# Sixty-four gathered row operations spread over a matmul pass, the final add and scale cut into halves, and four slots for rounded blocks

## The chip, the cores and the metric

The kernel runs on one core of a Trainium2 chip. The metric is the device time of one execution in microseconds (us); lower is better. The names of the engines are those of the profile: PE is TensorE (PEld its weight loads), DVE is VectorE, ACT is ScalarE, POOL is GpSimd, SP is SyncE.

## The reference, cut to what matters

The whole is one decoder layer over 256 tokens of width 2048: three attention branches, an output projection, and then a channel mixer with a table of 16384 experts, and a last RMSNorm. Only the mixer's value side and the norm are touched:

```python
def peer_ffn(h, w_q, sub_keys, u_tab, v_tab):
    ...                      # 8 heads x 16 chosen experts for each token: experts, g
    def chunk(args):
        xc, ec, gc = args
        a = jax.nn.gelu(jnp.einsum("td,thkd->thk", xc, u_tab[ec]))
        return jnp.einsum("thk,thkd->td", gc * a, v_tab[ec])
...
x = x + peer_ffn(rmsnorm(x, g_ffn[l]), ...)
return rmsnorm(x, g_final)   # y = x * rsqrt(mean(x*x) + EPS) * g
```

## The kernel before

The tokens are two tiles of 128 (t = 0 and 1), and a tile's (head, 16 experts) pairs are units, 16 in all. For 12 units the coefficient of each chosen expert is put into a dense matrix `ct` of 128 x 128 coefficients per token, and their value side is a dense product, the value pass: all 16384 rows of the table `peer_v` are read in 128 blocks of 128 rows. For the 4 last units, all of tile 1, the rows are gathered instead, 16 of `peer_u` and 16 of `peer_v` for each token and unit: 128 late operations, numbered n = 0 to 127. The first 64 are dot products (L1413), the last 64 add a gathered row times its coefficient to the residual `x1f[1]` (L1419). Here they are called dots and row operations. They stand inside the value pass.

In the value pass, for a block b:

- SP issues the load of block b into `v_raw[b % 4]` (L560) once block b-4 is used up (`acc_ok`).
- ACT rounds it to `v_hi` (L1064) and the coefficients to `c_hi` (L1087). `v_hi` and `c_hi` have two slots (`NHL`), so ACT waits until block b-2 is used up: `wait(act, acc_ok, b - 1)`.
- DVE subtracts: `v_lo` (in the place of `v_raw`, L1424), `c_lo` (L1426), and then does the late operations that the table `OPS_AT` gives to block b.
- PE does 24 matmuls of 128x512 (L1761): for each token tile t, for each of four column groups c, the three products hi*hi, hi*lo, lo*hi. All eight PSUM banks accumulate over the 128 blocks. Blocks 4 to 123 are a loop of four blocks a turn.
- POOL issues the gather of late operation n into one of four row slots (L641) when operation n-4 is done.

The table gives operation n >= 12 to block n + 4, and what would lie beyond block 127 to a last entry, which DVE works off behind its loop:

```python
for n in range(2 * LATE_OPS):
    b = n + n // 3 if n < 12 else min(n + 4, PKEYS)
    OPS_AT[b].append(n)
```

So operation 123 is in block 127, and 124 to 127 stand behind the loop. Then comes the end: for each tile DVE adds PSUM to `x1f[t]` (L1443, 2048 columns, on `fin_pe`), ACT squares and sums it (L1096), DVE and ACT work out 1/sqrt(mean + EPS) from it in small operations (L1107 to L1117 on DVE, L702 on ACT), and DVE multiplies into `outst[t]` in two halves (L1448), which SP stores (L582). At block 35 SP also loads the residuals of both tiles into `x1f` (L575).

Of the kernel before, what the change touches and what calls it, by code (L numbers as in the profile page):

```python
# [44 lines left out]
PH, PKEYS, PTOP = 8, 128, 16  # L45
EPS = 1e-6
# [20 lines left out]
NRAW, NHL = 4, 2  # L67
# [26 lines left out]
RING = 4  # L94
# [4 lines left out]
LATE_GROUPS = PTOP * (N_EARLY - PH) // GTOK  # L99
LATE_OPS = N_LATE * PTOP  # L100
V_FEW = 16
OPS_AT = {b: [] for b in range(PKEYS + 1)}
for n in range(2 * LATE_OPS):
    b = n + n // 3 if n < 12 else min(n + 4, PKEYS)
    OPS_AT[b].append(n)


# [80 lines left out]
def build(nc, x, rel_bias, g_mix, w_in, a_sinks, c_lat_gain, c_w_uk, c_w_uv, w_br_a, w_br_b, w_br_c,  # L188
# [5 lines left out]
    def at(name, kib, shape, dt=F32):  # L194
        return nc.alloc_sbuf_tensor_at(name, shape, dt, offset=base + int(kib * K))
# [24 lines left out]
    stat = at("stat", 205.0625, [P, 7, 8])  # L220
# [34 lines left out]
    ct = at("ct", 0, [P, NT, PKEYS, P])  # L255
# [35 lines left out]
    pickT = at("pickT", 205.46875, [P, 3, P])  # L291
    iota_f = at("iota_f", 206.96875, [P, P])

    ROW_AT, V_AT, VH_AT = (128, 168, 0, 64), (176, 192, 184, 160), (144, 152)
    row_ring = [at(f"row_ring{i}", kib, [P, D]) for i, kib in enumerate(ROW_AT)]
    v_raw = [at(f"v_raw{i}", kib, [P, D]) for i, kib in enumerate(V_AT)]
    v_lo = [at(f"v_lo{i}", kib, [P, D], FR) for i, kib in enumerate(V_AT)]
    v_hi = [at(f"v_hi{i}", kib, [P, D], FR) for i, kib in enumerate(VH_AT)]
    c_hi = [at(f"c_hi{i}", kib, [P, NT, P], FR) for i, kib in enumerate((205.46875, 202.0625))]
    c_lo = [at(f"c_lo{i}", kib, [P, NT, P], FR) for i, kib in enumerate((206.46875, 204))]  # L300
    x1f = [at(f"x1f{t}", kib, [P, D]) for t, kib in enumerate((72, 8))]
    gfin = at("gfin", 16, [P, D])
    outst = [at(f"outst{t}", kib, [P, D]) for t, kib in enumerate((80, 24))]

    ps = ctx.enter_context(nc.psum_tensor("ps", [P, 8, 512], F32))
    J, S_BANK, O_BANK, T_BANK, PT_BANK = 0, 2, 4, 5, 6
# [20 lines left out]
    lo_done = sem("lo_done")  # L327
    blk_done = sem("blk_done")
    evac_done = sem("evac_done")
    SSQ = {0: 1, 1: 2, 2: 3, 5: 4, 6: 5}  # L330
    sq_ok = sem("sq_ok")
    ssq_ok = sem("ssq_ok")
    ve_ok = sem("ve_ok")
    rt_ok = sem("rt_ok")
# [63 lines left out]
    ch_ok = sem("ch_ok")  # L398
# [26 lines left out]
    vh_ok = sem("vh_ok")  # L425
# [6 lines left out]
    o_ok = sem("o_ok")  # L432
# [255 lines left out]
    def _(act):  # L688
# [371 lines left out]

        def high_v(b):
            act.wait_ge(v_in[b % RING], 16 * (b // RING + 1))
            wait(act, acc_ok, b - 1)
            nc.scalar.activation(v_hi[b % NHL][:, :], v_raw[b % RING][:, :], ACT.Copy).then_inc(vh_ok, 1)  # L1064

        for b in range(NHL):
            high_v(b)
# [16 lines left out]
        for b in range(PKEYS):  # L1084
            if b >= NHL:
                high_v(b)
            nc.scalar.activation(c_hi[b % NHL][:, :, :], ct[:, :, b], ACT.Copy).then_inc(ch_ok, 1)  # L1087
            for n in OPS_AT[b - 1] if b else ():
                if n < LATE_OPS and n % PTOP == PTOP - 1:
                    squared(N_EARLY + n // PTOP)  # L1090
                    tanh_of(N_EARLY + n // PTOP)

        nc.scalar.activation(one_root[:, :], one_col[:, :], ACT.Sqrt)
        for t in range(NT):
            act.wait_ge(sum_ok, t + 1)
            nc.scalar.activation(outst[t][:, :], x1f[t][:, :], ACT.Square, accum_out=stat[:, 5 + t, 0:1]).then_inc(ssq_ok, 1)  # L1096
            root(5 + t, 1)


# [1 line left out]
    def _(dve):  # L1101
        def mean_root(q, cols, count, summed=False):

            s = stat[:, q]
            if not summed:
                dve.wait_ge(ssq_ok, SSQ[q])
            nc.vector.tensor_scalar(s[:, 2:2 + cols], s[:, 0:cols], 1.0 / count, EPS, ALU.mult, ALU.add).then_inc(ve_ok, 1)  # L1107
            dve.wait_ge(rt_ok, q + 1)
            nc.vector.reciprocal(s[:, 6:6 + cols], s[:, 4:4 + cols])
            dve.drain()  # L1110
            nc.vector.tensor_tensor(s[:, 4:4 + cols], s[:, 6:6 + cols], s[:, 6:6 + cols], ALU.mult)
            dve.drain()
# [328 lines left out]
        for t in range(NT):
            dve.wait_ge(fin_pe, t + 1)
            nc.vector.tensor_tensor(x1f[t][:, :], x1f[t][:, :], ps[:, 4 * t:4 * t + 4, :].rearrange("p a b -> p (a b)"), ALU.add).then_inc(sum_ok, 1)  # L1443
        for t in range(NT):
            mean_root(5 + t, 1, D)
            for h in range(2):
                cols = slice(D // 2 * h, D // 2 * (h + 1))
                nc.vector.scalar_tensor_tensor(out=outst[t][:, cols], in0=x1f[t][:, cols], scalar=stat[:, 5 + t, 6:7], in1=gfin[:, cols],  # L1448
                                               op0=ALU.mult, op1=ALU.mult).then_inc(o_ok, 1)


    @block.tensor
    def _(pe):
# [319 lines left out]


# [21 lines left out]
```

## Time and profile before

| what | us |
|---|---|
| median of 3 runs | 2097.63 |
| lowest and highest run | 2091.3, 2100.59 |
| the profiled execution | 2097.23 |
| its span | 2095.9 |

The span is the part of the profiled execution between its first and last recorded instruction. Times in the profile count from the span's start. The value pass begins at 1351.7 us and its last matmul at 2073.89 us. Clocks of PE are given as a share of full speed. An idle time in square brackets stands before an instruction, with what ended it.

### The profile page before, as it was taken

How to read it: one execution, taken by the hardware profiler on the slowest of the kernel's cores; microseconds unless marked ns; L12 is line 12 of the kernel's file. 1: busy time of each engine (PE TensorE's matmuls, PEld its weight loads, DVE VectorE, ACT ScalarE, POOL GpSimd, SP SyncE). 2: the span in 40 equal slices, each digit the busy share in tenths (PEclk: the TensorE clock that was granted, in tenths of full speed). 3: DMA queues.
4: the chain of work that ended last, by engine and by line, in shares of the span. 5: the costliest groups of instructions: out<-in, count | busy, mean ns of one | idle time of the engine just before them, and what ended most of it. 6: DMA issues, size and time to landing. Idle time of an engine off the chain costs nothing.

```text
span 2095.9 us, 27844 instructions
## 1 busy us (share of the span) xinstructions
PE 1790.6 (85%) x10780; PEld 1590.0 (76%) x10780; DVE 1551.0 (74%) x2043; ACT 856.1 (41%) x1312; POOL 477.7 (23%) x438
## 2 busy tenths in 40 slices
PE   7999999999999989656655235699999999999995
PEld 6999999999998877555644234588878888888884
DVE  5464444444565449999999999877878888888988
ACT  5444444444443421022222877534334334343342
POOL 0000000010053013453333767012211222212211
PEclk9999999999999999877877555799999999999998
DMA  9555555555467569989999899289999999999995
GB/s 312 158 168 168 168 170 171 171 171 166 143 189 281 191 232 418 422 363 426 392 382 395 336 397 426 96 333 351 393 378 367 392 375 381 381 380 372 369 387 212
DMA packets 293540, 627.82 MB, mean 300 GB/s; under 512 B 10365, under 2 KB 223406, under 8 KB 234959
## 3 DMA queue, kind: packets, MB, share of 16 engines
q0 software_dynamic: 48400, 343.95, 40.9%
q1 hardware_dynamic: 244558, 282.20, 39.5%
q8 instruction: 47, 0.77, 0.1%
q10 hardware_dynamic: 496, 0.58, 0.1%
q14 instruction: 39, 0.31, 0.0%
HBM read 622.45 MB, written 8.44 MB: 301 GB/s over the span
## 4 chain that ended last, share of the span: by engine, by line
PE 66%; DVE 19%; DVEq 5%; issue 4%; DMA 3%; ACT 1%; POOL 1%; another core or an unknown queue 1%; SPq 0%; POOLq 0%; ACTq 0%
PE ps L1761 33%; PE ps L1464 23%; DVE u_ring L1346 10%; DVEq L1301 4%; PE ps L1624 4%; PE ps L1646 2%; DMA u_ring<-in_peer_u,idx_all 2%; DMA v_raw<-in_peer_v 1%; DVE ones_d L1378 1%; DVE ones L1378 1%; PE ps L1569 1%; PE ps L1550 1%; PE ps L1559 0%; DVE pick L1334 0%
## 5 line engine op out<-in xcount | busy, mean ns | idle before, releaser
L1123 DVE TENSOR_TENSOR w_lo<-raw,w_hi 128x2048 fp32r<-128x2048 f32 x112 | 259.1, 2313 | 331.2 <-ACT w_hi L697 331.1
L1464 PE MATMUL ps<-act_hi,w_hi 128*128 128x256 f32 x1536 | 440.3, 287 | 4.9 <-DVE act_lo L1248 2.9
L1464 PE MATMUL ps<-act_hi,w_lo 128*128 128x256 f32 x1536 | 434.6, 283 | 0.0
L1464 PE MATMUL ps<-act_lo,w_hi 128*128 128x256 f32 x1536 | 434.5, 283 | 0.0
L1064 ACT ACTIVATE v_hi<-v_raw 128x2048 fp32r<-128x2048 f32 x128 | 245.3, 1917 | 423.6 <-PE ps L1761 414.9
L1761 PE MATMUL ps<-v_hi,c_hi 128*128 128x512 f32 x1024 | 406.6, 397 | 6.7 <-DVE c_lo L1426 6.7
L1761 PE MATMUL ps<-v_hi,c_lo 128*128 128x512 f32 x1024 | 405.5, 396 | 0.0
L1761 PE MATMUL ps<-v_lo,c_hi 128*128 128x512 f32 x1024 | 403.3, 394 | 0.0
L1346 DVE CUSTOM_DVE_ANT_0 u_ring<-u_ring,ps 128x2048 f32<-128x2048 f32 x159 | 359.8, 2277 | 14.6 <-DMA u_ring<-in_peer_u,idx_all 14.3
L1424 DVE TENSOR_TENSOR v_lo<-v_raw,v_hi 128x2048 fp32r<-128x2048 f32 x128 | 293.7, 2294 | 94.1 <-ACT v_hi L1064 94.0
L697 ACT ACTIVATE w_hi<-raw 128x2048 fp32r<-128x2048 f32 x112 | 214.1, 1911 | 262.5 <-PE ps L1464 217.8
L1464 PEld LDWEIGHTS ps<-act_hi,w_hi 128*128 128x128 f32 x1536 | 294.5, 192 | 6.1 <-issue 4.0
L1464 PEld LDWEIGHTS ps<-act_lo,w_hi 128*128 128x128 f32 x1536 | 294.6, 192 | 0.3 <-issue 0.2
L1464 PEld LDWEIGHTS ps<-act_hi,w_lo 128*128 128x128 f32 x1536 | 294.4, 192 | 0.0
L641 POOL DMA_INDIRECT u_ring<-in_peer_u,idx_all x192 | 187.8, 978 | 285.8 <-DVE early_dots L1346 198.8
L1761 PEld LDWEIGHTS ps<-v_hi,c_hi 128*128 128x128 f32 x1024 | 192.8, 188 | 54.2 <-DVE c_lo L1426 4.9
L1761 PEld LDWEIGHTS ps<-v_lo,c_hi 128*128 128x128 f32 x1024 | 192.8, 188 | 47.7
L1761 PEld LDWEIGHTS ps<-v_hi,c_lo 128*128 128x128 f32 x1024 | 192.9, 188 | 44.3
L1419 DVE SCALAR_TENSOR_TENSOR x1f<-row_ring,cw_all,x1f 128x2048 f32<-128x2048 f32 x64 | 150.5, 2351 | 6.9 <-issue 0.9
L641 POOL DMA_INDIRECT row_ring<-in_peer_u,idx_all x64 | 73.6, 1150 | 338.1 <-DVE late_dots L1413 321.8
L1413 DVE CUSTOM_DVE_ANT_0 row_ring<-row_ring,h 128x2048 f32<-128x2048 f32 x64 | 146.2, 2284 | 0.0
L641 POOL DMA_INDIRECT row_ring<-in_peer_v,idx_all x64 | 81.3, 1270 | 277.9 <-DVE x1f L1419 257.7
(225 smaller groups left out, 2095.5 us busy)
## 6 DMA issues: line engine op xcount, KB each, us to landing
v_raw<-in_peer_v SPq DMA_DIRECT2D x128, 1024.0 KB, 7.0
raw<-in_w_in SPq DMA_DIRECT2D x80, 1024.0 KB
raw<-in_w_out SPq DMA_DIRECT2D x16, 1024.0 KB
wq_raw<-in_peer_w_q SPq DMA_DIRECT2D x8, 2048.0 KB, 19.0
raw<-in_w_br_a SPq DMA_DIRECT2D x16, 512.0 KB
bias_by_query<-bias_by_distance POOLq DMA_DIRECT2D x1, 4096.0 KB, 21.1
bias_st<-bias_by_query POOLq DMA_DIRECT2D x16, 256.0 KB, 4.7
raw<-in_w_br_b SPq DMA_DIRECT2D x16, 256.0 KB
```

What stands on the lines that cost most here:

```text
L641: return pool.indirect_dma_start(dst, None, table, bass.IndirectOffsetOnAxis(ap=idx_all[:, PTOP * unit + k:PTOP * unit + k + 1], axis=0))
L697: nc.scalar.activation(w_hi[:, j % NHL], raw[:, j % NRAW], ACT.Copy).then_inc(hi_done, 1)
L1064: nc.scalar.activation(v_hi[b % NHL][:, :], v_raw[b % RING][:, :], ACT.Copy).then_inc(vh_ok, 1)
L1123: nc.vector.tensor_tensor(w_lo[:, j % NHL], raw[:, j % NRAW], w_hi[:, j % NHL].bitcast(F32), ALU.subtract).then_inc(lo_done, 1)
L1301: dve.drain()
L1346: nc.vector.tensor_tensor_reduce(out=u_ring[:, slot], in0=u_ring[:, slot], in1=h2p[u // PH], scale=0.5, scalar=0.0, op0=ALU.mult, op1=ALU. ...
L1413: nc.vector.tensor_tensor_reduce(out=row_ring[slot][:, :], in0=row_ring[slot][:, :], in1=h2[:, 1], scale=0.5, scalar=0.0, op0=ALU.mult, op ...
L1419: nc.vector.scalar_tensor_tensor(out=x1f[1][:, :], in0=row_ring[slot][:, :], scalar=cw_all[:, PTOP * unit + k:PTOP * unit + k + 1], in1=x1 ...
L1424: nc.vector.tensor_tensor(v_lo[b % RING][:, :], v_raw[b % RING][:, :], v_hi[b % NHL][:, :].bitcast(F32), ALU.subtract)
L1464: last = nc.tensor.matmul(out_ap, w_parts[wp][:, slot, k], act_parts[ap][:, k], start=(k == k0 and m == 0), stop=(k == k1 - 1 and m == 2))
L1624: last = nc.tensor.matmul(ps[:, 2 * (c % 2) + t, :], mg_parts[ap][:, T * k + P * t:T * k + P * t + P], w_wide[wp][:, j % NHL, kk], start=( ...
L1761: last = nc.tensor.matmul(ps[:, 4 * t + c, :], c_parts[cp][j % NHL][:, t], v_parts[vp][j % v_slots[vp]][:, WIDE * c:WIDE * c + WIDE], star ...
```

## The change

The table gives operations 64 to 127 places that come 0 to 6 blocks earlier, `n + 4 - (n - 64) // 10`: every ninth block from 77 on (77, 86, 95, 104, 113, 122) takes two row operations instead of one, the last operation is in block 125, and none stands behind the loop. From block 64 on `v_hi`, `c_hi` and `c_lo` have four slots instead of two; the new ones lie where coefficients of used-up blocks were. PE's loop over the blocks becomes two loops, one for each count of slots. The output tiles move to places of row slots 0 and 1. At the end `fin_pe` counts half tiles, DVE adds half tiles, ACT squares half tiles into two sums, and DVE's small operations are put in between; one of them fewer stands in the root, and one more in the mean.

```diff
-OPS_AT = {b: [] for b in range(PKEYS + 1)}
+OPS_AT = {b: [] for b in range(PKEYS)}
 for n in range(2 * LATE_OPS):
-    b = n + n // 3 if n < 12 else min(n + 4, PKEYS)
+    b = n + n // 3 if n < 12 else n + 4 - max(n - LATE_OPS, 0) // 10
     OPS_AT[b].append(n)
...
-    ROW_AT, V_AT, VH_AT = (128, 168, 0, 64), (176, 192, 184, 160), (144, 152)
+    ROW_AT, V_AT, VH_AT = (128, 168, 0, 64), (176, 192, 184, 160), (144, 152, 80, 24)
...
-    c_hi = [at(f"c_hi{i}", kib, [P, NT, P], FR) for i, kib in enumerate((205.46875, 202.0625))]
-    c_lo = [at(f"c_lo{i}", kib, [P, NT, P], FR) for i, kib in enumerate((206.46875, 204))]
+    c_hi = [at(f"c_hi{i}", kib, [P, NT, P], FR) for i, kib in enumerate((205.46875, 202.0625, 88, 89))]
+    c_lo = [at(f"c_lo{i}", kib, [P, NT, P], FR) for i, kib in enumerate((206.46875, 204, 90, 91))]
...
-    outst = [at(f"outst{t}", kib, [P, D]) for t, kib in enumerate((80, 24))]
+    outst = [at(f"outst{t}", kib, [P, D]) for t, kib in enumerate((128, 168))]
...
+    def hi_slot(b):
+
+        return b % NHL if b < PKEYS // 2 else b % RING
+
...
-            wait(act, acc_ok, b - 1)
-            nc.scalar.activation(v_hi[b % NHL][:, :], v_raw[b % RING][:, :], ACT.Copy).then_inc(vh_ok, 1)
+            wait(act, acc_ok, b - 1 if b < PKEYS // 2 + NHL else max(b - RING + 1, PKEYS // 2))
+            nc.scalar.activation(v_hi[hi_slot(b)][:, :], v_raw[b % RING][:, :], ACT.Copy).then_inc(vh_ok, 1)
...
-            act.wait_ge(sum_ok, t + 1)
-            nc.scalar.activation(outst[t][:, :], x1f[t][:, :], ACT.Square, accum_out=stat[:, 5 + t, 0:1]).then_inc(ssq_ok, 1)
+            for h in range(2):
+                cols = slice(D // 2 * h, D // 2 * (h + 1))
+                act.wait_ge(sum_ok, 2 * t + h + 1)
+                nc.scalar.activation(outst[t][:, cols], x1f[t][:, cols], ACT.Square, accum_out=stat[:, 5 + t, h:h + 1]).then_inc(ssq_ok, 1)
             root(5 + t, 1)
...
-        for n in OPS_AT[PKEYS]:
-            late_op(n)
...
+        def add_half(t, h):
+
+            cols = slice(D // 2 * h, D // 2 * (h + 1))
+            dve.wait_ge(fin_pe, 2 * t + h + 1)
...
+        add_half(0, 0)
+        add_half(0, 1)
+        add_half(1, 0)
+        mean_square(0)
+        add_half(1, 1)
+        inverse_root(0)
+        out_half(0, 0)
+        mean_square(1)
+        out_half(0, 1)
+        inverse_root(1)
+        out_half(1, 0)
+        out_half(1, 1)
...
-        add_block(0, first=True)
-        with pe.Fori(1, PKEYS // RING - 1) as i:
-            add_block(i)
-        add_block(PKEYS // RING - 1, final=True)
+        add_block(0, (NHL, RING), first=True)
+        with pe.Fori(1, PKEYS // RING // 2) as i:
+            add_block(i, (NHL, RING))
+        with pe.Fori(PKEYS // RING // 2, PKEYS // RING - 1) as i:
+            add_block(i, (RING, RING))
+        add_block(PKEYS // RING - 1, (RING, RING), final=True)
```

The first place is DVE around block 77, operations 72 to 75. The digit in a name is its slot: `x1f1` is the residual of tile 1, `row_ring0` to `row_ring3` are the row slots. Before:

```order
L1419 SCALAR_TENSOR_TENSOR x1f1_155<-row_ring0_136,cw_all_118,x1f1_155 128x2048 [waits row_in0]
L1424 TENSOR_TENSOR v_lo1_145<-v_raw1_141,v_hi1_149 128x2048 [waits vh_ok]
L1426 TENSOR_TENSOR c_lo1_153<-ct_99,c_hi1_151 128x256 [waits ch_ok]
L1419 SCALAR_TENSOR_TENSOR x1f1_155<-row_ring1_137,cw_all_118,x1f1_155 128x2048 [waits row_in1]
L1424 TENSOR_TENSOR v_lo2_146<-v_raw2_142,v_hi0_148 128x2048 [waits vh_ok]
L1426 TENSOR_TENSOR c_lo0_152<-ct_99,c_hi0_150 128x256 [waits ch_ok]
L1419 SCALAR_TENSOR_TENSOR x1f1_155<-row_ring2_138,cw_all_118,x1f1_155 128x2048 [waits row_in2]
```

After:

```order
L1425 SCALAR_TENSOR_TENSOR x1f1_161<-row_ring0_136,cw_all_118,x1f1_161 128x2048 [waits row_in0]
L1430 TENSOR_TENSOR v_lo1_145<-v_raw1_141,v_hi1_149 128x2048 [waits vh_ok]
L1432 TENSOR_TENSOR c_lo1_157<-ct_99,c_hi1_153 128x256 [waits ch_ok]
L1425 SCALAR_TENSOR_TENSOR x1f1_161<-row_ring1_137,cw_all_118,x1f1_161 128x2048 [waits row_in1]
L1425 SCALAR_TENSOR_TENSOR x1f1_161<-row_ring2_138,cw_all_118,x1f1_161 128x2048 [waits row_in2]
L1430 TENSOR_TENSOR v_lo2_146<-v_raw2_142,v_hi2_150 128x2048 [waits vh_ok]
L1432 TENSOR_TENSOR c_lo2_158<-ct_99,c_hi2_154 128x256 [waits ch_ok]
```

Two row operations stand between the `c_lo` of block 77 and the `v_lo` of block 78, and block 78 has slot 2 of `v_hi` instead of slot 0.

The second place is DVE at the end of its program, from the `v_lo` of block 127 to the last output. Before:

```order
L1424 TENSOR_TENSOR v_lo3_147<-v_raw3_143,v_hi1_149 128x2048 [waits vh_ok]
L1426 TENSOR_TENSOR c_lo1_153<-ct_99,c_hi1_151 128x256 [waits ch_ok]
L1419 SCALAR_TENSOR_TENSOR x1f1_155<-row_ring3_139,cw_all_118,x1f1_155 128x2048 [waits row_in3]
L1419 SCALAR_TENSOR_TENSOR x1f1_155<-row_ring0_136,cw_all_118,x1f1_155 128x2048 [waits row_in0]
L1419 SCALAR_TENSOR_TENSOR x1f1_155<-row_ring1_137,cw_all_118,x1f1_155 128x2048 [waits row_in1]
```

After (the row operation at the top is 127, in block 125):

```order
L1425 SCALAR_TENSOR_TENSOR x1f1_161<-row_ring3_139,cw_all_118,x1f1_161 128x2048 [waits row_in3]
L1430 TENSOR_TENSOR v_lo2_146<-v_raw2_142,v_hi2_150 128x2048 [waits vh_ok]
L1432 TENSOR_TENSOR c_lo2_158<-ct_99,c_hi2_154 128x256 [waits ch_ok]
L1430 TENSOR_TENSOR v_lo3_147<-v_raw3_143,v_hi3_151 128x2048 [waits vh_ok]
L1432 TENSOR_TENSOR c_lo3_159<-ct_99,c_hi3_155 128x256 [waits ch_ok]
```

Five row operations, 123 to 127, stood between the last `c_lo` and the first add (the last two of them are left out above), and now none does. The operations in the adds' and outputs' part stand in the order that the diff's last twelve calls on DVE show.

## Rows read from the trace of the kernel before

**Rows 1.** The page: span, and its chain that ended last, by line.

```profile
span 2095.9 us, 27844 instructions
...
PE ps L1761 33%; PE ps L1464 23%; DVE u_ring L1346 10%; DVEq L1301 4%; PE ps L1624 4%; PE ps L1646 2%; DMA u_ring<-in_peer_u,idx_all 2%; DMA v_raw<-in_peer_v 1%; DVE ones_d L1378 1%; DVE ones L1378 1%; PE ps L1569 1%; PE ps L1550 1%; PE ps L1559 0%; DVE pick L1334 0%
```

**Rows 2.** The chain in order of time, from 1380 us: start, length, what.

```profile
1379.80 158.35 PE ps L1761 x679
...
1538.17 16.61 DMA v_raw<-in_peer_v
...
1559.42 503.72 PE ps L1761 x2160
```

**Rows 3.** Timeline of DVE, end of the value pass and after it.

```profile
2065.18 2.29 DVE L1424 TENSOR_TENSOR v_lo<-v_raw,v_hi 128x2048 fp32r<-128x2048 f32 x1 [0.49 <-ACT v_hi L1064]
2067.39 0.42 DVE L1426 TENSOR_TENSOR c_lo<-ct,c_hi 128x256 fp32r<-128x256 f32 x1
2067.90 9.68 DVE L1419 SCALAR_TENSOR_TENSOR x1f<-row_ring,cw_all,x1f 128x2048 f32<-128x2048 f32 x4
2078.00 2.35 DVE L1419 SCALAR_TENSOR_TENSOR x1f<-row_ring,cw_all,x1f 128x2048 f32<-128x2048 f32 x1 [0.42 <-DMA row_ring<-in_peer_v,idx_all]
2080.44 4.48 DVE L1443 TENSOR_TENSOR x1f<-x1f,ps 128x2048 f32<-128x2048 f32 x2
...
2089.59 0.16 DVE L1109 RECIPROCAL stat<-stat 128x1 f32<-128x1 f32 x1 [0.27 <-ACT stat L702]
2089.83 0.16 DVE L1111 TENSOR_TENSOR stat<-stat 128x1 f32<-128x1 f32 x1
...
2090.76 2.48 DVE L1448 SCALAR_TENSOR_TENSOR outst<-x1f,stat,gfin 128x1024 f32<-128x1024 f32 x2
```

**Rows 4.** Timeline of PE at three matmuls of the last two blocks.

```profile
2062.74 0.40 PE L1761 MATMUL ps<-v_lo,c_hi 128*128 128x512 f32 x1
...
2068.57 0.40 PE L1761 MATMUL ps<-v_hi,c_hi 128*128 128x512 f32 x1
...
2073.89 0.39 PE L1761 MATMUL ps<-v_lo,c_hi 128*128 128x512 f32 x1
```

**Rows 5.** Timeline of ACT: the last rounding, a square, its sum, a root.

```profile
2063.23 1.92 ACT L1064 ACTIVATE v_hi<-v_raw 128x2048 fp32r<-128x2048 f32 x1 [3.33 <-PE ps L1761]
...
2082.76 1.91 ACT L1096 ACTIVATE outst<-x1f 128x2048 f32<-128x2048 f32 x1 [15.79 <-DVE x1f L1443]
2084.58 0.19 ACT L1096 ACTIVATION_READ_ACCUMULATOR outst<-x1f 128x1 f32 x1
...
2089.36 0.20 ACT L702 ACTIVATE stat<-stat 128x1 f32<-128x1 f32 x1 [2.24 <-DVE stat L1107]
```

**Rows 6.** Groups of DVE by line, 1740 to 2096 us.

```profile
L1419 DVE SCALAR_TENSOR_TENSOR x1f<-row_ring,cw_all,x1f 128x2048 f32<-128x2048 f32 x64 | 150.5, 2351 | 6.9 <-issue 0.9 <-DMA row_ring<-in_peer_v,idx_all 0.4
L1424 DVE TENSOR_TENSOR v_lo<-v_raw,v_hi 128x2048 fp32r<-128x2048 f32 x59 | 135.5, 2296 | 28.4 <-ACT v_hi L1064 28.3
```

**Rows 7.** Loads of `v_raw` issued from 1700 us on: issue to landing.

```profile
DMA to landing us min/median/max: 4.7/6.9/9.8
```

**Rows 8.** Gathers into `row_ring`, 1740 to 2060 us: issue to landing.

```profile
DMA to landing us min/median/max: 5.4/7.4/12.1
```

**Rows 9.** Stretches: length, busy times, PE clock, DMA share, GB/s.

```profile
1745.00:2067.00 322.00, 322.00 (x1388) 259.98 (x1387) 288.09 (x173) 130.28 (x118) 69.52 (x58) 1.00 0.95 372
...
1534.00:1556.00 22.00, 20.93 (x90) 16.50 (x88) 14.55 (x12) 6.50 (x7) 3.79 (x4) 1.00 1.00 417
```

**Rows 10.** Timeline of PE around its one wait in the pass.

```profile
1554.53 0.40 PE L1761 MATMUL ps<-v_lo,c_hi 128*128 128x512 f32 x1
1559.42 0.50 PE L1761 MATMUL ps<-v_hi,c_hi 128*128 128x512 f32 x1 [4.49 <-DVE c_lo L1426]
...
1560.08 0.63 PE L1761 MATMUL ps<-v_lo,c_hi 128*128 128x512 f32 x1
1560.51 0.63 PE L1761 MATMUL ps<-v_hi,c_hi 128*128 128x512 f32 x1
```

More of the change, by code:

```diff
@@ L329, in build @@
     evac_done = sem("evac_done")
-    SSQ = {0: 1, 1: 2, 2: 3, 5: 4, 6: 5}
+    SSQ = {0: 1, 1: 2, 2: 3, 5: 5, 6: 7}
     sq_ok = sem("sq_ok")
@@ L1086, in _ @@
                 high_v(b)
-            nc.scalar.activation(c_hi[b % NHL][:, :, :], ct[:, :, b], ACT.Copy).then_inc(ch_ok, 1)
+            nc.scalar.activation(c_hi[hi_slot(b)][:, :, :], ct[:, :, b], ACT.Copy).then_inc(ch_ok, 1)
             for n in OPS_AT[b - 1] if b else ():
@@ L1423, in _ @@
             dve.wait_ge(vh_ok, b + 1)
-            nc.vector.tensor_tensor(v_lo[b % RING][:, :], v_raw[b % RING][:, :], v_hi[b % NHL][:, :].bitcast(F32), ALU.subtract)
+            nc.vector.tensor_tensor(v_lo[b % RING][:, :], v_raw[b % RING][:, :], v_hi[hi_slot(b)][:, :].bitcast(F32), ALU.subtract)
             dve.wait_ge(ch_ok, b + 1)
-            nc.vector.tensor_tensor(c_lo[b % NHL][:, :, :], ct[:, :, b], c_hi[b % NHL][:, :, :].bitcast(F32), ALU.subtract).then_inc(vl_ok, 1)
+            nc.vector.tensor_tensor(c_lo[hi_slot(b)][:, :, :], ct[:, :, b], c_hi[hi_slot(b)][:, :, :].bitcast(F32), ALU.subtract).then_inc(vl_ok, 1)
             for n in OPS_AT[b - 2] if b > 1 else ():
@@ L1440, in _ @@
         dve.drain()
[L1441 to L1449, printed above, removed]
+        def add_half(t, h):
+            cols = slice(D // 2 * h, D // 2 * (h + 1))
+            dve.wait_ge(fin_pe, 2 * t + h + 1)
+            nc.vector.tensor_tensor(x1f[t][:, cols], x1f[t][:, cols], ps[:, 4 * t + 2 * h:4 * t + 2 * h + 2, :].rearrange("p a b -> p (a b)"),
+                                    ALU.add).then_inc(sum_ok, 1)
@@ new lines, in mean_square, with inverse_root @@
+        def mean_square(t):
+            s = stat[:, 5 + t]
+            dve.wait_ge(ssq_ok, SSQ[5 + t])
+            nc.vector.tensor_scalar(s[:, 3:4], s[:, 0:1], s[:, 1:2], 1.0 / D, ALU.add, ALU.mult)
+            dve.drain()
+            nc.vector.tensor_scalar(s[:, 2:3], s[:, 3:4], EPS, None, ALU.add).then_inc(ve_ok, 1)
+        def inverse_root(t):
+            s = stat[:, 5 + t]
+            dve.wait_ge(rt_ok, 6 + t)
+            nc.vector.reciprocal(s[:, 6:7], s[:, 4:5])
+            dve.drain()
+            nc.vector.scalar_tensor_tensor(out=s[:, 4:5], in0=s[:, 6:7], scalar=s[:, 6:7], in1=s[:, 2:3], op0=ALU.mult, op1=ALU.mult)
+            dve.drain()
+            nc.vector.tensor_scalar(s[:, 4:5], s[:, 4:5], -0.5, 1.5, ALU.mult, ALU.add)
+            dve.drain()
+            nc.vector.tensor_tensor(s[:, 6:7], s[:, 6:7], s[:, 4:5], ALU.mult)
+            dve.drain()
@@ new lines, in out_half @@
+        def out_half(t, h):
+            cols = slice(D // 2 * h, D // 2 * (h + 1))
+            nc.vector.scalar_tensor_tensor(out=outst[t][:, cols], in0=x1f[t][:, cols], scalar=stat[:, 5 + t, 6:7], in1=gfin[:, cols],
+                                           op0=ALU.mult, op1=ALU.mult).then_inc(o_ok, 1)
+        add_half(0, 0)
[6 more added lines that the diff above has]
+        mean_square(1)
@@ L1751, in _, with add_block @@
         v_parts, c_parts = (v_hi, v_lo), (c_hi, c_lo)
-        v_slots = (NHL, RING)
-        def add_block(i, first=False, final=False):
+        def add_block(i, v_slots, first=False, final=False):
             for j in range(RING):
@@ L1760, in add_block @@
                         for m, (vp, cp) in enumerate(PRODUCTS):
-                            last = nc.tensor.matmul(ps[:, 4 * t + c, :], c_parts[cp][j % NHL][:, t],
+                            last = nc.tensor.matmul(ps[:, 4 * t + c, :], c_parts[cp][j % v_slots[0]][:, t],
                                                     v_parts[vp][j % v_slots[vp]][:, WIDE * c:WIDE * c + WIDE],
                                                     start=(first and j == 0 and m == 0), stop=(final and j == RING - 1 and m == 2))
-                    if final and j == RING - 1:
-                        last.then_inc(fin_pe, 1)
+                        if final and j == RING - 1 and c % 2:
+                            last.then_inc(fin_pe, 1)
                 if not (final and j == RING - 1):
                     last.then_inc(acc_ok, 1)
-        add_block(0, first=True)
-        with pe.Fori(1, PKEYS // RING - 1) as i:
-            add_block(i)
-        add_block(PKEYS // RING - 1, final=True)
+        add_block(0, (NHL, RING), first=True)
[4 more added lines that the diff above has]
+        add_block(PKEYS // RING - 1, (RING, RING), final=True)
 _INS = ["x", "rel_bias", "g_mix", "w_in", "a_sinks", "c_lat_gain", "c_w_uk", "c_w_uv", "w_br_a", "w_br_b", "w_br_c",
```

## The prediction, made before the changed kernel was run

> **What bounds the kernel now.** I read the page's chain first, to find the stage: the value pass, line 1761 on PE, holds 33% of it [rows 1]. The change touches this pass and what follows, so I read the chain in order of time from there. It stays on PE with one break: at 1538 us the chain goes over a load of `v_raw` that took 16.61 us to land, and from 1559.42 us on PE works 503.72 us, 2160 matmuls, with nothing in between [rows 2]. That is 0.233 us a matmul and 5.58 us a block, as the first matmul of block 127 at 2068.57 and the last of block 125 at 2062.74 also say (24 steps and one) [rows 4]. In this half of the pass PE waits for nobody, so whatever feeds it sooner brings nothing by itself. Four slots and earlier gathers can only keep something from going wrong here.
>
> The gain must come from the end. The last matmul starts at 2073.89 [rows 4]. A result of PE is seen by another engine 0.49 us after the start of the last matmul: the one at 2062.74 releases ACT at 2063.23 [rows 4, 5]. So the last sum could be read at 2074.38. But DVE is busy with row operations 123 to 127 from 2067.90 to 2080.35, and starts its two adds at 2080.44 [rows 3]. Its 0.42 us wait for the gather is inside that. The adds end at 2084.92, the outputs at 2093.24 (two from 2090.76, 2.48 us), and the span at 2095.9, 2.66 us of store later [rows 1, 3].
>
> **Part 1: row operations out of the end.** Five of them, 12.0 us, leave the stretch in front of the adds. What decides then is PE, not DVE, since DVE has only `v_lo` and `c_lo` left in block 127. The first add no longer starts at 2080.44; the last may start at 2074.38. That is worth 2080.44 - 2074.38 = 6.06 us.
>
> **Part 2: half tiles.** In block 127 the 6th, 12th, 18th and 24th matmul close a half tile: at a step of 0.232 us from 2068.57, and with the 0.49 us, at 2070.2, 2071.6, 2073.0 and 2074.38. A half add costs at least half of 2.24 us (4.48 for two), 1.12, and at most what a half output costs, 1.24 [rows 3]; I take 1.15, as it is the same kind of operation as the 2.24. Three of the halves and `mean_square(0)` then run under PE: the third ends at 2074.15. `mean_square` is two dependent small operations, at the step of 0.24 us that the rows of the root show (2089.59 to 2089.83), 0.48 together. Its squares are ready: half of 1.91 and 0.19 for reading the sum [rows 5] is 1.15 behind 2072.75, so 2073.9. It ends at 2074.63, 0.25 later than PE, and the last half add at 2075.78. So instead of 4.48 us of adds 1.15 remain: +3.33, less the 0.25.
>
> **Part 3: behind the adds.** `inverse_root` has four small operations where five took 2089.59 to 2090.76, so 0.96. Then: root of tile 0 to 2076.74, output half 1.24 to 2077.98, mean of tile 1 to 2078.46, half to 2079.70, root to 2080.66, two halves to 2083.14. ACT's root of tile 1, 0.20 us [rows 5], lies under the half output before it; uncovered it would be 0.2 to 0.5 us. This is 7.36 us where before it was 8.32 (2084.92 to 2093.24): +0.96. The store is unchanged, 2.66 us, and the span ends at 2085.8.
>
> **Part 4: what the earlier row operations cost in the pass.** In a block DVE has 2.3 + 0.34 + 2.35 us and gaps, and 28.4 us of idle time before 59 `v_lo`, 0.48 each [rows 6]. `c_lo` of block 127 ends at 2067.81, 0.76 us before PE wants it [rows 3, 4]. A second row operation brings 2.40 us (0.05 of it a gap). With two slots that would be 2.40 - 0.48 - 0.76 = 1.16 us of PE, six times 7.0 us. With four slots `v_hi` of a block may be made as soon as `v_raw` has landed. The load is issued 3 blocks, 16.7 us, before PE wants the block; rounding to `c_lo` takes 2063.23 to 2067.81, 4.58 us; with the 0.49 us of release and a landing of 6.9 us [rows 7], `c_lo` can be ready 4.8 us ahead, and with the longest landing, 9.8 us, 1.8 us ahead. Between two such blocks lie nine blocks with 0.48 us of slack, 4.3 us, more than the 2.40. So DVE stands some 3 to 5 us ahead at such a block and falls back by 2.4: cost nothing, or 0.6 us at a place where the longest landing falls on it. I take zero. POOL's gather of operation n waits for n-4, some 3 blocks or 16 us before it is used, against landings of 7.4 us and at most 12.1 [rows 8]: covered too.
>
> DMA carries 2.1 MB a block instead of 2: gathers 68 to 127 are released from block 68 to 122, 60 in 54 blocks, so 1.11 gathers and one load of 1.049 MB each in 5.58 us, 397 GB/s. Before, the stretch moved 372 at a share of 0.95; the highest 22 us of this pass moved 417 at a share of 1.00 [rows 9]. So 397 fits, with 5% to spare. The HBM Reference of the Trainium skill (its section of specifications) gives a core some 358 GB/s as its part of the bandwidth, which would forbid it, and says of a core alone that it measures about 425. The rows of 372 and 417 agree with the second figure only; by the first the pass would be bound by transfers before the change already.
>
> **Part 5: the rest.** One more loop start on PE I take as a turn of the loop: the 2160 matmuls of [rows 2] hold 22 such turns and still average 0.233 us, so zero; if a start cost as much as three matmuls, it would be 0.7 us. Moving buffers costs nothing that a row shows. PE's step itself is 0.2332 before the break and 0.2323 behind it (158.35 / 679; 503.72 less the slower matmuls of the fallen clock, over 2160), and nothing in the program says why, so up to 1.4 us either way over 1500 matmuls stays open.
>
> **Sum.** 6.06 + 3.33 - 0.25 + 0.96 = 10.1 us. Against the profiled execution, 2097.23, that is 2087.1. That execution lies 0.4 us below the median of 2097.63. In ratio it is 0.48% to 0.50%, so it falls on the very bound of 0.5% that I call about what a measurement of this kernel can tell.
>
> **Rivals.**
>
> *The four slots don't hide the second row operation.* DVE may not get ahead, if landings lengthen with the denser gathers. Against it: landing of 6.9 us at a share of 0.95. For it: with two queues competing at 1534 us loads took 16.61. PE then loses up to 1.16 us at six blocks, and 10.1 shrinks to 3.1: 2094. Chance 0.11.
>
> *The transfers give no more than before.* If 372 GB/s is the limit and not the demand, each of the six gathers brought forward costs 1.049 MB / 372 GB/s = 2.8 us of PE, 16.9 in all, and each such wait can lower the clock: behind the wait of 4.49 us PE's step was 0.43 instead of 0.23 us for nine matmuls, about 1.8 us [rows 10]. That gives 2097.2 - 10.1 + 16.9 = 2104, and up to 2115 with the clock lost six times: slower. It decides from a demand above the limit on, that is if less than 397 GB/s can be had over many blocks. The 417 row speaks against it. Chance 0.05. The page of the Trainium skill named above (HBM Reference, specifications) would put the limit lower still, at some 358 GB/s.
>
> *The break at 1538 us falls out otherwise.* It is a load of block 36 behind the two residual loads; nothing in the change touches it. But a wait of 4.49 us and 1.8 us of clock is as large as the gain, and the runs of before differ by 9 us. If the runs of after miss it, the time is near 2081; if two such come, 2093. Chance 0.08 and 0.05.
>
> *The change does only half of it:* the halves' order makes DVE wait for ACT's sums at every step, so parts 2 and 3 bring nothing. Each wait is then at most 1.15 + 0.2 us; 2091.5. For it: the square's sum is read separately, 0.19 us. Chance 0.05.
>
> **How the numbers follow.** The forecast, gain of 8.7 to 11.5 us, 2085.7 to 2088.5, has 0.66. The cases above hold 0.34. For the range I leave out the transfers' case and half of the one at 2081, and add the 1.4 us of the step: 2082 to 2095. Faster by over 0.5% means a gain over 10.5 us: a little under half of 0.66, with the case at 2081: 0.40. Within 0.5%: the rest of the forecast and the cases from 2091 to 2094: 0.53. Slower: 0.07.
>
> **What would show it.** In the profile after: the first half add starts under PE, about 1.6 us after block 127 begins, and the last half add 0.5 to 0.8 us after the last matmul starts; from there to the end 10 to 11 us. No wait of PE from block 64 on. Idle time of DVE before `v_lo` falls by about 14 us (six times 2.4), and it waits for rounding less often at blocks behind 77, 86 and so on. ACT in the second half waits for loads, not for PE. DMA moves about 395 GB/s. The prediction is wrong if PE waits for `c_lo` in the second half, if the loads' median landing goes over 10 us, or if something other than `fin_pe` releases the last add.

## The result, and the profile after

| what | before | changed |
|---|---|---|
| median, us (5 runs each) | 2097.26 | 2082.52 |
| lowest and highest | 2091.3, 2100.59 | 2076.41, 2084.84 |
| span of the profiled execution | 2095.9 | 2082.7 |

The ratio is 0.9923, with a 95% interval of 0.9902 to 0.9943. The changed kernel is 0.8% faster; 2087.1 had been predicted, and "within 0.5%" as the likeliest. The medians differ by 14.7 us, and runs of one kernel differ by 8 to 9 us among themselves.

The two spans differ by 13.2 us. Two marks divide each into three stretches, read from PE's timeline: the first matmul of block 64 (1717.22 before, 1717.91 after), and the last matmul (2073.89 and 2070.76):

| stretch | before | changed | difference |
|---|---|---|---|
| start to block 64 | 1717.22 | 1717.91 | +0.7 |
| second half of the value pass | 356.67 | 352.85 | -3.8 |
| from the last matmul's start to the end | 22.01 | 11.94 | -10.1 |

The chain of the changed kernel in order of time, to be held against [rows 2]:

```profile
1354.76 187.74 PE ps L1800 x792
1542.52 13.84 DMA v_raw<-in_peer_v
...
1561.01 311.39 PE ps L1800 x1344
1872.42 10.04 DMA v_raw<-in_peer_v
...
1894.54 175.26 PE ps L1800 x762
2069.83 1.22 DVE x1f L1448
```

It passes to DVE ahead of PE's last matmul, with the third half add, which works on what the 18th of block 127's 24 matmuls closed; the last half add then stands behind DVE's own small operations and not behind PE. The pass began 3.1 us later than before, and the wait at block 36 was 2.8 us shorter; both lie ahead of anything that the change touches. The seven steps of 0.43 us behind the wait of before [rows 10] are absent too, and at the start of the pass the changed kernel has 13 such steps against 6.

DVE at the end, against [rows 3]:

```profile
2060.77 0.42 DVE L1432 TENSOR_TENSOR c_lo<-ct,c_hi 128x256 fp32r<-128x256 f32 x1
2067.11 3.94 DVE L1448 TENSOR_TENSOR x1f<-x1f,ps 128x1024 f32<-128x1024 f32 x3 [5.92 <-PE ps L1800]
...
2071.60 0.15 DVE L1457 TENSOR_SCALAR stat<-stat 128x1 f32<-128x1 f32 x1 [0.43 <-issue]
2071.67 1.21 DVE L1448 TENSOR_TENSOR x1f<-x1f,ps 128x1024 f32<-128x1024 f32 x1
...
2073.79 1.28 DVE L1475 SCALAR_TENSOR_TENSOR outst<-x1f,stat,gfin 128x1024 f32<-128x1024 f32 x1
...
2077.53 2.48 DVE L1475 SCALAR_TENSOR_TENSOR outst<-x1f,stat,gfin 128x1024 f32<-128x1024 f32 x2
```

DVE is idle for 5.92 us and waits for PE, where before DVE was the late one. PE's last matmul:

```profile
2070.76 0.39 PE L1800 MATMUL ps<-v_lo,c_hi 128*128 128x512 f32 x1
```

The last half add starts 0.91 us behind the start of that matmul; the outputs end at 2080.0 and the span at 2082.7.

The second half of the pass, against [rows 9] and [rows 7]: a stretch, and the loads of `v_raw` in it.

```profile
1721.00:2040.00 319.00, 318.87 (x1389) 260.23 (x1388) 299.96 (x188) 128.63 (x119) 144.79 (x64) 1.00 0.99 398
```

```profile
DMA to landing us min/median/max: 6.3/8.7/10.0
```

Before moved 377 GB/s in the same stretch, at a share of 0.96. PE waited once in this half, for the `c_lo` of block 96, behind a load that took 10.04 us:

```profile
1894.54 0.19 PEld L1800 LDWEIGHTS ps<-v_hi,c_hi 128*128 128x128 f32 x1 [0.55 <-DVE c_lo L1432]
```

It cost 0.28 us: block 95 took 5.73 us, where others of its slot took 5.45.

Now the part that was not forecast. First matmuls of blocks 100 to 104, before:

```profile
1917.98 0.39 PE L1761 MATMUL ps<-v_hi,c_hi 128*128 128x512 f32 x1
...
1923.57 0.40 PE L1761 MATMUL ps<-v_hi,c_hi 128*128 128x512 f32 x1
...
1929.13 0.39 PE L1761 MATMUL ps<-v_hi,c_hi 128*128 128x512 f32 x1
...
1934.73 0.40 PE L1761 MATMUL ps<-v_hi,c_hi 128*128 128x512 f32 x1
```

and in the changed kernel:

```profile
1916.76 0.39 PE L1800 MATMUL ps<-v_hi,c_hi 128*128 128x512 f32 x1
...
1922.36 0.40 PE L1800 MATMUL ps<-v_hi,c_hi 128*128 128x512 f32 x1
...
1927.90 0.39 PE L1800 MATMUL ps<-v_hi,c_hi 128*128 128x512 f32 x1
...
1933.35 0.39 PE L1800 MATMUL ps<-v_hi,c_hi 128*128 128x512 f32 x1
...
1938.79 0.39 PE L1800 MATMUL ps<-v_hi,c_hi 128*128 128x512 f32 x1
```

Before, blocks took 5.59, 5.56, 5.60 us. Now they take 5.60, 5.54, 5.45, 5.44: the blocks in the two old slots are as they were, and those in the two new slots are shorter, at the same full clock (1.00 in both). Nothing waits in any of them. Averaged over blocks 100 to 123 the four took 5.597, 5.556, 5.598 and 5.556 us before and 5.597, 5.548, 5.440 and 5.448 after: 0.16 and 0.11 us less in the new slots.

### The profile page after: what moved, and what is told of

It reads as the page before. It is cut to its first block, busy times and chain, and to the rows that moved or that the text cites. A ratio compares the mean times of both kernels' runs of the same rounds, so it can differ in the third digit from the quotient of the medians.

```text
span 2082.7 us, 27851 instructions
## 1 busy us (share of the span) xinstructions
PE 1784.3 (86%) x10780; PEld 1586.9 (76%) x10780; DVE 1548.7 (74%) x2045; ACT 856.4 (41%) x1316; POOL 539.6 (26%) x438
## 4 chain that ended last, share of the span: by engine, by line
PE 65%; DVE 20%; DVEq 5%; issue 4%; DMA 3%; ACT 1%; POOL 1%; another core or an unknown queue 1%; SPq 0%; POOLq 0%; ACTq 0%
PE ps L1800 32%; PE ps L1504 23%; DVE u_ring L1352 10%; DVEq L1307 4%; PE ps L1664 4%; PE ps L1686 2%; DMA u_ring<-in_peer_u,idx_all 2%; DMA v_raw<-in_peer_v 1%; DVE ones_d L1384 1%; DVE ones L1384 1%; PE ps L1609 1%; PE ps L1590 1%; PE ps L1599 1%; DVE pick L1340 1%
## 5 line engine op out<-in xcount | busy, mean ns | idle before, releaser
L645 POOL DMA_INDIRECT row_ring<-in_peer_v,idx_all x64 | 146.0, 2282 | 179.4 <-DVE x1f L1425 160.8
```

The costliest lines, as they stand in the source:

```text
L645: return pool.indirect_dma_start(dst, None, table, bass.IndirectOffsetOnAxis(ap=idx_all[:, PTOP * unit + k:PTOP * unit + k + 1], axis=0))
```

## The experiments

Theory A: PE's matmuls are paced by where their operands lie, and the new slots lie better. Rivals: the shorter step belongs to the dealt-out order, or to DVE's lead, or to chance. Beside it the terms of the forecast were each taken alone. Ratios are against before, with their 95% interval. "End" is the time from the start of the last matmul to the end of the span, "second half" that from block 64 to the last matmul, both of the profiled execution.

**Four slots alone.** Before, with `hi_slot`, the wait, the places of the slots and PE's two loops of the change:

```diff
-            wait(act, acc_ok, b - 1)
+            wait(act, acc_ok, b - 1 if b < PKEYS // 2 + NHL else max(b - RING + 1, PKEYS // 2))
```

> Before, with four slots from block 64 on and nothing else of the change: row operations 124 to 127 stay behind the loop, tiles stay whole. In the changed kernel PE's block took 5.60, 5.55, 5.44 and 5.45 us by slot in the second half, where before took 5.60 and 5.55. Theory A (the step of PE depends on where the new slots lie): the same four numbers here, second half shorter by about 4.0 us, the end unchanged at some 22 us behind the last matmul, total about 4 us under before. Rival R1 (the shorter step came from the order of the row operations, or is luck of that execution): blocks of 5.60 and 5.55 in all slots, total within 1 us of before, leaving out what the wait at block 35 does.

2090.57 us, ratio 0.9958 (0.9941 to 0.9974), more gain than the 4 us expected. The blocks by slot took 5.597, 5.548, 5.440 and 5.448 us, second half 352.4: theory A's four numbers, so the order of the row operations is not the cause, nor a chance of one execution. But the end was 18.7 us and not 22. DVE's last blocks here:

```profile
2060.39 2.29 DVE L1428 TENSOR_TENSOR v_lo<-v_raw,v_hi 128x2048 fp32r<-128x2048 f32 x1
...
2063.10 9.68 DVE L1423 SCALAR_TENSOR_TENSOR x1f<-row_ring,cw_all,x1f 128x2048 f32<-128x2048 f32 x4
2073.13 2.35 DVE L1423 SCALAR_TENSOR_TENSOR x1f<-row_ring,cw_all,x1f 128x2048 f32<-128x2048 f32 x1 [0.35 <-DMA row_ring<-in_peer_v,idx_all]
```

The last `v_lo` starts at 2060.39 with no idle time, 6.8 us ahead of its block (2067.19), where before it was 3.4 ahead [rows 3, 4]. So DVE begins the five row operations 3.3 us earlier against PE. This expectation of an unchanged end missed because I had left DVE's lead out of it.

**Half tiles alone.** Before, with the end of the change:

```diff
-                    if final and j == RING - 1:
...
+                        if final and j == RING - 1 and c % 2:
...
+        add_half(0, 0)
...
```

> Before, with the half tiles at the end and nothing else. By the forecast's terms the five row operations still stand ahead of the first add at 2080.4 us, so that four half adds (4.5 us) and one mean (0.5) take the place of 4.5 us, and the 8.3 us behind the adds become 7.4: gain 0.4 us, nothing that can be told. Rival: halves are worth their full 4 us (3.3 + 0.96 less 0.25) also behind the row operations: 2093.

2097.55 us, ratio 0.9998 (0.9984 to 1.0011); end 21.7 us against 22.0, so 0.3 us where 0.4 was expected: the halves are worth next to nothing while DVE comes late. The weights lay where they lie in before, and yet slot 1 took 5.60 us to the end and the second half 358.2, 1.5 more than in the profile of before.

**Two slots throughout, with the rest of the change.**

```diff
-        return b % NHL if b < PKEYS // 2 else b % RING
+        return b % NHL
...
-            wait(act, acc_ok, b - 1 if b < PKEYS // 2 + NHL else max(b - RING + 1, PKEYS // 2))
+            wait(act, acc_ok, b - 1)
...
```

PE's two loops are one again, with two slots.

> The changed kernel with two slots throughout. Forecast's rival made real: at blocks 78, 87, 96, 105, 114 and 123 PE waits 1.16 us each for the c_lo, 7.0 us in all, and the end keeps its 10.1 us: 3.1 us under before. PE's blocks are 5.60 and 5.55 again, so the changed kernel's 4 us are missing too: some 11 us over the changed kernel. If DVE's slack of 0.48 us and the 0.76 us of lead hide the second operation after all: no waits, 10.1 us under before.

2094.89 us, ratio 0.9988 (0.9976 to 1.0001). PE behind block 77:

```profile
1794.29 0.39 PE L1800 MATMUL ps<-v_lo,c_hi 128*128 128x512 f32 x1
1795.69 0.50 PE L1800 MATMUL ps<-v_hi,c_hi 128*128 128x512 f32 x1 [1.01 <-DVE c_lo L1432]
```

The gap between the two starts is 1.40 us instead of 0.23, and there are six of them, 1.34 to 1.40, at blocks 78, 87, 96, 105, 114 and 123: 6.8 us lost in all, 1.13 each, against 1.16 forecast. The end is 11.9 us. So dealing out needs the slots; without them six waits give back 6.8 of 10.1 us. The total is 12.4 us over the changed kernel, 11 forecast; behind the first of these waits slot 1 took 5.60 us a block in most stretches and not 5.55.

**Whole tiles, with the rest of the change.**

```diff
-        add_half(0, 0)
-        add_half(0, 1)
...
+        for t in range(NT):
+            dve.wait_ge(fin_pe, t + 1)
...
```

> The changed kernel without the half tiles: row operations dealt out and four slots stay. Adds of whole tiles on fin_pe of each tile: first from 12 matmuls into block 127, second starts 0.49 us after the last matmul's start and takes 2.24, then 8.3 us and a store of 2.7. So 13.7 us from the last matmul's start to the end instead of 11.9: 1.8 us over the changed kernel, 12 us under before. Rival (the halves bring their full 4.0 us only if DVE is free, and it is): 4.0 us over the changed kernel.

2084.4 us, ratio 0.9939 (0.9923 to 0.9954), 1.9 us over the changed kernel by medians, whose intervals overlap; the profile is clearer: end 13.7 us, the expected value, against 11.9. The blocks by slot were 5.597, 5.548, 5.440 and 5.448 again.

**Which operand it is.** Three runs move one operand each in the second half. First the coefficients of slots 0 and 1 beside those of 2 and 3:

```diff
-    c_hi = ... enumerate((205.46875, 202.0625, 88, 89))]
-    c_lo = ... enumerate((206.46875, 204, 90, 91))]
+    c_hi = ... enumerate((205.46875, 202.0625, 88, 89, 92, 93))]
+    c_lo = ... enumerate((206.46875, 204, 90, 91, 94, 95))]
...
+    C_SECOND = (4, 5, 2, 3)
```

> The changed kernel, with c_hi and c_lo of blocks b % 4 = 0 and 1 of the second half moved too, to 92 to 95 KiB beside the other two pairs; v_hi stays. Theory A1 (the place of c, the weights, sets PE's step): all four slots take 5.44 to 5.45 us, the second half 62 x 0.13 / 2 = 4 us less again, total about 4 us under the changed kernel. Theory A2 (the place of v_hi sets it): slots 0 and 1 stay at 5.60 and 5.55, no change.

2079.83 us, ratio 0.9919 (0.9906 to 0.9932). First matmuls of blocks 100 to 104:

```profile
1912.41 0.39 PE L1806 MATMUL ps<-v_hi,c_hi 128*128 128x512 f32 x1
...
1917.85 0.39 PE L1806 MATMUL ps<-v_hi,c_hi 128*128 128x512 f32 x1
...
1923.29 0.39 PE L1806 MATMUL ps<-v_hi,c_hi 128*128 128x512 f32 x1
...
1928.73 0.39 PE L1806 MATMUL ps<-v_hi,c_hi 128*128 128x512 f32 x1
...
1934.17 0.39 PE L1806 MATMUL ps<-v_hi,c_hi 128*128 128x512 f32 x1
```

All take 5.44 us, though `v_hi` stays where it was; second half 347.9 us, 4.9 less than in the changed kernel (4 expected). It is the place of the coefficients, the weights of the matmul.

Then the new coefficient slots, shifted by 32 bytes:

```diff
+    c_hi = ... enumerate((205.46875, 202.0625, 88.03125, 89.03125))]
+    c_lo = ... enumerate((206.46875, 204, 90.03125, 91.03125))]
```

> The changed kernel with the new c slots (b % 4 = 2 and 3 of the second half) shifted by 32 bytes, so that they begin at an odd multiple of 32 bytes as slot 0 does, and nothing else moved. Theory A1a (it is the alignment of c): blocks of slots 2 and 3 go from 5.44 to 5.60 us, second half 31 x 0.155 = 4.8 us longer, total about 5 us over the changed kernel. Theory A1b (it is the region of c) or A2 (v_hi): slots 2 and 3 stay at 5.44, no change.

2086.95 us, ratio 0.9952 (0.9939 to 0.9965).

```profile
1918.71 0.40 PE L1800 MATMUL ps<-v_hi,c_hi 128*128 128x512 f32 x1
...
1924.31 0.40 PE L1800 MATMUL ps<-v_hi,c_hi 128*128 128x512 f32 x1
...
1929.87 0.39 PE L1800 MATMUL ps<-v_hi,c_hi 128*128 128x512 f32 x1
...
1935.46 0.40 PE L1800 MATMUL ps<-v_hi,c_hi 128*128 128x512 f32 x1
...
1941.06 0.40 PE L1800 MATMUL ps<-v_hi,c_hi 128*128 128x512 f32 x1
```

Slots 2 and 3 take 5.59 and 5.60 us, second half 357.4 us, where before took 356.7. A shift by 32 bytes takes the whole unforecast gain away. The four slots and their timing are those of the changed kernel, so DVE's lead is not the cause either.

Third, `v_hi` places exchanged between the slots:

```diff
+    def vh_slot(b):
+
+        return b % NHL if b < PKEYS // 2 else (b + 2) % RING
```

> The changed kernel with v_hi's places exchanged in the second half: blocks b % 4 = 0 and 1 use 80 and 24 KiB, 2 and 3 use 144 and 152; c slots as in the changed kernel. Theory A2 (place of v_hi): now slots 0 and 1 take 5.44 and 2 and 3 take 5.60 and 5.55; total the same. Theory A1 (place of c): slots keep 5.60, 5.55, 5.44, 5.45. Total the same in both; the look at the blocks decides.

2082.79 us, ratio 0.9932 (0.9919 to 0.9944). The blocks by slot: 5.597, 5.548, 5.440, 5.448, unchanged. Which of its four places `v_hi` has plays no part. All four are multiples of 8 KiB, so an odd start address of the moving operand was not tried.

**Which start address.** A coefficient tile starts at 16896 bytes plus its KiB. In before, slot 0 starts at 480 bytes beyond a multiple of 512 (both tiles), slot 1 at 64 (`c_hi`) and 0 (`c_lo`); the new slots at 0. Before, with slot 0 alone moved by 32 bytes, to a remainder of 448:

```diff
+    c_hi = ... enumerate((205.4375, 202.0625))]
+    c_lo = ... enumerate((206.4375, 204))]
```

> Before, with c_hi and c_lo of slot 0 moved by 32 bytes down (205.4375 and 206.4375 KiB), so that both begin at a multiple of 64 bytes, and nothing else. Theory A1a (alignment): even blocks, 5.60 us in before, go to 5.55 or, as both are now at multiples of 64, to 5.44; 0.04 to 0.16 us at 63 blocks, so 2.5 to 10 us under before. Theories A1b and A2: no change, 2097.

2091.97 us, ratio 0.9985 (0.997 to 0.9999). Slot 0 went from 5.597 to 5.493 us, between the two values expected; slot 1 took 5.547 in the second half (5.556 before); both halves of the pass gain. The measured gain, 0.15%, is at the low end. The twelve runs lie between 2087.0 and 2101.2 us, and the profiled one is the fastest of them; it came out 10.2 us under the one of before: 8.2 in the first 64 blocks, of which 3.4 are a shorter wait at block 36, 3.6 in the second half, less a start of the pass 1.7 us later.

Before, with slot 0 at a remainder of 384 and slot 1 at 0:

```diff
+    c_hi = ... enumerate((205.375, 202))]
+    c_lo = ... enumerate((206.375, 204))]
```

> Before, with its four c tiles at multiples of 128 bytes (slot 0: 205.375 and 206.375 KiB) and of 512 bytes (slot 1: 202 and 204 KiB), and nothing else. So far tiles at an odd multiple of 32 bytes gave a block of 5.60 us, at an odd multiple of 64 bytes 5.49 to 5.55, at multiples of 512 bytes 5.44. If the start address alone sets the step: slot 1 takes 5.44 us, slot 0 5.44 to 5.49, in both halves of the pass; 124 blocks x about 0.14 = 17 us under before, less what PE then waits for c_lo, whose lead of 0.76 us shrinks by 0.15 a block where DVE (5.07 us a block) still keeps up. Rival (only the region below 96 KiB is fast): slot 1 stays at 5.55, total as in the run with slot 0 at multiples of 64.

2086.56 us, ratio 0.9957 (0.9943 to 0.9971). Slot 1 took 5.457 us, above 200 KiB as well, in both halves, so the region is not the cause. Slot 0, although at a multiple of 128 bytes, took 5.589, more than at 448. So my expectation of 17 us failed by the half that rested on slot 0. The same four addresses in the changed kernel:

```diff
-    c_hi = ... enumerate((205.46875, 202.0625, 88, 89))]
-    c_lo = ... enumerate((206.46875, 204, 90, 91))]
+    c_hi = ... enumerate((205.375, 202, 88, 89))]
+    c_lo = ... enumerate((206.375, 204, 90, 91))]
```

> The changed kernel with the same addresses for c slots 0 and 1, its slots 2 and 3 as they are (multiples of 512 bytes). The start address theory: all blocks 5.44 to 5.49 us, so 8 to 10 us less in the first half and 4 less in the second, 12 to 14 us under the changed kernel, about 27 under before. It falls short if PE begins to wait: DMA would have to carry 2.1 MB in 5.44 us, 405 GB/s, and the loads of the residuals would hit a faster pass.

2072.09 us (4 runs), ratio 0.9887 (0.9867 to 0.9907): the lowest median of all, 10 us under the changed kernel's; the forecast was 12 to 14, and slot 0 (5.59) again gave nothing. PE waited twice, at blocks 36 and 105, 2.0 us in all. And with the residual loads of block 35 six blocks apart:

```diff
-                for t in range(NT):
-                    sp.dma_start(x1f[t][:, :], x1_d[:, t, :]).then_inc(res_in[t], 16)
+            for t in range(NT):
+                if n == 2 * V_FEW + RING - 1 + 6 * t:
+                    sp.dma_start(x1f[t][:, :], x1_d[:, t, :]).then_inc(res_in[t], 16)
```

> The kernel of the run before, with the second of the two residual loads issued six blocks later than the first, instead of right behind it. If the wait of PE at block 36 (2.1 to 4.9 us between two matmuls so far, each time at the same place) comes from two loads of 1 MB ahead of block 36 in one queue, it vanishes or falls below 1 us: 2 to 5 us less, and the runs lie closer together. If it comes from the gathers beside it, it stays.

2074.36 us (4 runs), ratio 0.9893 (0.9872 to 0.9914), no difference to the run before it, where 2 to 5 us less were expected. The wait at block 36 was absent in its profile, but it was absent too in two profiles where the loads are together: with slot 0 at 384 on the kernel before, and in the next run. So whether spreading them removes it stays open.

Last, the changed kernel with three further remainders in one execution, and only one run of it:

```diff
+    c_hi = ... enumerate((205.46875, 202.0625, 90.125, 92.25, 94.375, 88.0625))]
+    c_lo = ... enumerate((206.46875, 204, 91.125, 93.25, 204, 89.0625))]
...
+    C_SECOND = (0, 5, 2, 3)
```

> The changed kernel, where in the second half the c tiles of each slot start at another remainder of 512 bytes: slot 0 480 (as it was), slot 1 64, slot 2 128, slot 3 256, the last three all below 96 KiB. Known so far: remainder 0 gives 5.44 to 5.46 us a block in both regions, 32 and 480 give 5.60, 384 gave 5.59, 448 gave 5.49. If the step grows with the distance from a multiple of 512: slot 1 5.49, slot 2 5.59, slot 3 5.59 or more. If only multiples of 64 bytes and the region count, slots 1 to 3 take 5.44.

2078.63 us. Slots 0 to 3 took 5.60, 5.60, 5.58 and 5.45 us: remainders 480, 64, 128 and 256. Neither of the two expectations fits: the time does not grow with the distance from a multiple of 512, and below 96 KiB not every multiple of 64 is good. All block times together, by the remainder of 512 bytes at which both tiles start:

| remainder | 0 | 32 | 64 | 128 | 256 | 384 | 448 | 480 |
|---|---|---|---|---|---|---|---|---|
| us a block | 5.44 to 5.46 | 5.59 to 5.60 | 5.60 | 5.58 | 5.45 | 5.59 | 5.49 to 5.50 | 5.60 |

The two multiples of 256 bytes are the short ones, 448 lies between, and the others are long. 64, 128 and 256 rest on this one execution. Why 448 is better than 384 is open, and so is why the start address counts at all: the records of the weight loads last 187 to 188 ns in blocks 100 to 123 of the changed kernel, in all four slots.

Slot 1 of before is mixed: `c_hi` at 64, used by 16 of a block's 24 matmuls, and `c_lo` at 0, used by 8. With 0.2333 us for the first and 0.2267 for the second a block would take 5.55 us, my estimate, and 5.55 to 5.56 is what it often took. But it took 5.60 in other stretches, like the first 35 blocks of before and all of the run with half tiles alone. Where two slots alternate it changed only behind a wait of PE: in before at block 36, and in the run with two slots throughout at blocks 36, 78, 114 and 123, but not at the other waits. What decides between the two values is open. It is worth 0.04 us a block, or 1.4 us in a half of the pass where two slots alternate.

## Why the prediction was right and wrong

*What bounds the kernel, and where the gain must come from:* right that PE is the bound, and 10.1 us come from behind the last matmul, as summed: 10.07 measured. Not right that they are the only place: "The gain must come from the end" left out PE's own step.

*Part 1, the row operations:* right in kind. DVE waits 5.92 us for PE in front of the adds. The size of 6.06 is not what the part is worth by itself: with whole tiles the end fell from 22.0 to 13.7, by 8.3 us, since the add of tile 0 then runs under PE too. 3.3 of them the slots alone already gave.

*Part 2, the half tiles:* the mechanism is right, the share too large. Half adds take 1.21 us in the records (0.06 over my value), and the wait for the mean was longer, 0.91 us from the last matmul to the add instead of 0.74, since 0.43 us of issue time stand between the two small operations. Parts 2 and 3 counted 4.04 us for the halves; two runs measure 0.3 us alone and, by the ends of 13.7 and 11.9, 1.8 us with the rest. What is missing, 2.24, is the add of tile 0 that belongs to part 1. The sum of the parts is not touched by this. Rival "only half of it" fell.

*Part 3:* 7.13 us from the last add's end (2072.88) to the outputs' end (2080.01), against 7.36. This 0.23 too much and the 0.23 too little of part 2 (0.17 for the mean, 0.06 for the add) cancel, so that the sum of the end fits better than its terms.

*Part 4, the cost in the pass:* right but for 0.28 us. With two slots the price is 1.13 us at six blocks (1.16 forecast), with four it is covered: idle time of DVE before `v_lo` fell from 28.4 us [rows 6] to 14.5, ACT waits 196.3 us for loads and 3.4 for PE, and DMA moved 398 GB/s at a share of 0.99 (397 forecast). The rival in which 372 GB/s is the limit fell. The 358 GB/s that the HBM Reference of the Trainium skill gives a core (specifications) did not bind here: this trace moved 398 over 319 us. The same section's 425 for a core alone agrees: the fastest 22 us moved 426 before (1538 to 1560) and 425 in the changed kernel (1848 to 1870). The 417 of [rows 9] was not the highest of the pass, as I had called it. What I had not forecast is that the landing of a load grows to 8.7 us in the median, which leaves less lead. It is not the rate alone: with all coefficients at multiples of 512 bytes (402 GB/s) it was 7.6.

*The signs:* two of those that I had named for a wrong prediction came true in small. PE waited for `c_lo` in the second half, once, 0.28 us, within the 0.6 us that part 4 allowed. And the last half add was not released by `fin_pe` but stood behind the mean of tile 0, as part 2 itself had worked out, so this sign contradicted its own forecast.

*Part 5, "the rest":* this step failed. It put PE's step under the change at zero in the sum, with 1.4 us either way. "Moving buffers costs nothing that a row shows" was true of cost, but the new slots of the coefficients start at multiples of 512 bytes, and PE's matmul takes 0.2267 us there and 0.2333 in slot 0. I had seen the two steps, 0.2332 and 0.2323, and written that nothing in the program says why; it does, in the places of the coefficients. The change made it 3.8 us (5.3 against an execution like that of the half tiles alone, whose slot 1 takes 5.60), and single blocks of before would have shown 5.60 and 5.56 us in turn, by slot, from block 37 on.

*Sum and chances:* 10.1 lay 0.4 us below the bound of 0.5%, and I gave "within 0.5%" 0.53 against 0.40. The missing 3.8 us put the kernel beyond it; the measured median, 2082.52, lies inside the range of 2082 to 2095 only just. Of the 14.7 us between the medians the profiles explain 13.2 (10.1 and 3.8, less the 0.7 of the first half); the other 1.5 lie within what runs of one kernel differ by. The step's uncertainty had been entered in the range but not in the chances, where it counted most.

## What to carry to other kernels

When PE is the bound without a gap, look for gain behind its last instruction and in its step. For the first, ask what stands on the reading engine between PE's last delivery and the last result. Work that is dealt out into an engine's slack needs a buffer that covers one instruction of that work. And when a change moves or adds weight tiles of matmuls, compare the step of matmuls slot by slot: here 32 bytes of start address of a weight tile were worth 3% of the step, and no wait in the profile shows it.

## What was not expected of the hardware

Matmuls of 128x512 float32r with weight tiles of 128x128 four-byte elements, back to back at full clock, took 0.2267 us with weights starting at a multiple of 256 or 512 bytes and up to 0.2333 us elsewhere. The place of `v_hi`, the moving operand, did not matter between 24, 80, 144 and 152 KiB.

The start of the value pass, before which nothing was changed in any of these kernels, lay between 1351.6 and 1357.0 us in their profiles, and the wait at block 36 between none and 4.9 us from matmul to matmul. Behind the two longest of these waits (4.89 and 4.20 us) PE had seven and eight steps of 0.42 to 0.43 us, and behind those of 1.5 to 3.6 us none. Most of the 9 us by which the runs of one kernel differ can come from these; no experiment here shows it.
